# Seven half products for eight in the gate and up projections of a dense SwiGLU

## The reference, cut to what matters

```
h  = h + gated_deltanet(...)
hn = rms_norm(h, ffn_norm[0])                                  # (256, 1024)
h  = h + (silu(hn @ w_gate) * (hn @ w_up)) @ w_down            # w_gate, w_up (1024, 3584), w_down (3584, 1024)
...                                                            # layer 1: attention, then 8 experts
```

## Time and profile before

| | before |
|---|---|
| median of 3 runs (lowest to highest) | 1490.9 us (1490.5 to 1490.95) |
| span of the profiled execution | 1489.1 us |
| what lies around the span, median less span | 1.8 us |
| TensorE busy | 1477.0 us (99%) |
| VectorE, ScalarE, GpSimd busy | 1189.9, 947.9, 116.2 us |
| share of the chain that ended last | PE 96%, DVE 2%, DMA 1% |

### The profile page before, as it was taken

One profiled execution on the slowest core, in us unless ns is written; L12 is line 12 of the kernel. 1 busy time (PEld: TensorE's weight loads), 2 busy tenths in 40 slices (PEclk: granted clock), 3 DMA queues, 4 the chain that ended last, 5 costly groups with the idle time before them and its releaser, 6 DMA issues.

```text
span 1489.1 us, 20171 instructions
## 1 busy us (share of the span) xinstructions
PE 1477.0 (99%) x7900; PEld 1234.6 (83%) x7900; DVE 1189.9 (80%) x1056; ACT 947.9 (64%) x852; POOL 116.2 (8%) x77
## 2 busy tenths in 40 slices
PE   9999999999999999999999999999999999999998
PEld 7999988888887788888888888888888888888886
DVE  5977775444478699889889889898898988988985
ACT  4554544434465676777677777677777677767773
POOL 0470110000013000000000000000000000000000
PEclk9999999999999999999999999999999999999999
DMA  6331885555414299999999999999999999999990
GB/s 227 114 115 58 307 320 181 173 209 183 169 58 156 99 396 393 396 383 393 397 382 394 393 369 386 381 371 381 383 380 372 389 380 363 391 383 359 395 362 30
DMA packets 186696, 445.60 MB, mean 299 GB/s; under 512 B 5399, under 2 KB 5680, under 8 KB 186635
## 3 DMA queue, kind: packets, MB, share of 16 engines
q1 hardware_dynamic: 182208, 430.12, 77.7%
q0 software_dynamic: 3936, 14.20, 3.3%
q10 hardware_dynamic: 490, 0.42, 0.1%
HBM read 437.89 MB, written 7.89 MB: 299 GB/s over the span
## 4 chain that ended last, share of the span: by engine, by line
PE 96%; DVE 2%; DMA 1%; ACT 0%; POOL 0%; issue 0%; SPq 0%; DVEq 0%; ACTq 0%
PE bank L1482 14%; PE bank L1484 14%; PE bank L1483 14%; PE bank L1467 7%; PE bank L1469 7%; PE bank L1468 7%; PE bank L698 4%; PE bank L1145 3%; PE bank L1144 3%; PE bank L1143 3%; PE bank L785 2%; PE bank L789 2%; PE bank L790 2%; PE bank L791 2%; PE bank L1132 1%; PE bank L1130 1%
## 5 line engine op out<-in xcount | busy, mean ns | idle before, releaser
L2625 DVE TENSOR_TENSOR ring_r<-ring,buf_r 128x2048 fp32r<-128x2048 f32 x336 | 751.2, 2284 | 28.0 <-ACT buf_r L1926 28.0
L1926 ACT ACTIVATE buf_r<-ring 128x2048 fp32r<-128x2048 f32 x336 | 629.4, 1914 | 52.5 <-PE bank L1469 43.3
L1482 PE MATMUL bank<-ring_r,buf_r 128*128 128x512 f32 x896 | 354.5, 396 | 0.3 <-DVE buf_r L2745 0.3
L1484 PE MATMUL bank<-buf_r,buf_r 128*128 128x512 f32 x896 | 349.6, 390 | 0.0
L1483 PE MATMUL bank<-buf_r,buf_r 128*128 128x512 f32 x896 | 349.0, 389 | 0.0
L1484 PEld LDWEIGHTS bank<-buf_r,buf_r 128*128 128x128 f32 x896 | 168.0, 188 | 36.0
L1482 PEld LDWEIGHTS bank<-ring_r,buf_r 128*128 128x128 f32 x896 | 168.4, 188 | 33.6 <-DVE buf_r L2745 0.4
L1483 PEld LDWEIGHTS bank<-buf_r,buf_r 128*128 128x128 f32 x896 | 168.5, 188 | 33.4
L1467 PE MATMUL bank<-ring_r,buf_r 128*128 128x512 f32 x440 | 172.8, 393 | 0.1
L1469 PE MATMUL bank<-buf_r,buf_r 128*128 128x512 f32 x440 | 171.5, 390 | 0.0
L1468 PE MATMUL bank<-buf_r,buf_r 128*128 128x512 f32 x440 | 171.2, 389 | 0.0
(11 more groups left out here) (378 smaller groups left out, 1867.1 us busy)
## 6 DMA issues: line engine op xcount, KB each, us to landing
ring<-in_moe_w_gate SPq DMA_DIRECT2D x56, 2048.0 KB, 10.0
ring<-in_moe_w_up SPq DMA_DIRECT2D x56, 2048.0 KB, 10.4
ring<-in_moe_w_down SPq DMA_DIRECT2D x56, 2048.0 KB, 10.4
ring<-in_a_w_in SPq DMA_DIRECT2D x8, 2048.0 KB, 8.5
ring<-in_dense_w_gate SPq DMA_DIRECT2D x7, 2048.0 KB, 7.8
ring<-in_dense_w_up SPq DMA_DIRECT2D x7, 2048.0 KB, 7.9
ring<-in_dense_w_down SPq DMA_DIRECT2D x7, 2048.0 KB, 8.0
ring<-in_a_w_out SPq DMA_DIRECT2D x2, 2048.0 KB, 10.9
```

Of the source, the lines that this page charges most:

```text
L1482: pe.matmul(o, xh, low[:, c], start=k == 0, stop=False)
L1484: ins = pe.matmul(o, xh, high[:, c], start=False, stop=k == KT - 1)
L1926: act.activation(HB[m % NHB], half_words(m, U_MOE), ACT.Copy).then_inc(m_wh, 1)
L2625: dve.tensor_tensor(half_low(m, U_MOE), half_words(m, U_MOE), HB[m % NHB], ALU.subtract).then_inc(m_wl, 1)
```

## The change: what it does

The slices 3 to 6 are taken in pairs (3, 4) and (5, 6) (`MIXED`). For the gate of one pair, and for the up of one pair, the input is two token tiles by two halves of the 1024 input rows, and the weights are two halves by two slices. The plain way is eight half products. The new way is seven, by Strassen's method in the form with shared sums: seven weight matrices (three blocks as they are, four sums of blocks) times seven row matrices. Slices 1 and 2 (`PLAIN`) stay plain, in a new order. Dense now has 54 blocks (`NB`), 0 to 53, of 24 matmuls, or of 12 where they are one of the 28 products:

blocks 0 to 3 slice 0; 4 to 7 gates of 1 and 2; 8, 9 down 0; 10 to 13 ups of 1 and 2; **14 to 20** gate products of 3 and 4; 21, 22 down 1; **23 to 29** up products; 30, 31 down 2; **32 to 38** gate products of 5 and 6; 39, 40 down 3; **41 to 47** up products; 48 to 53 downs 4, 5, 6.

```diff
+def dense_blocks():
+    out = [("w", kind, 0, half) for kind in ("gate", "up") for half in range(2)]
+    for p in range(1, PAIRS + 1):
+        j = 2 * p - 1
+        for kind in ("gate", "up"):
+            if p in PLAIN:
+                out += [("w", kind, j + sl, half) for sl in range(2) for half in range(2)]
+            else:
+                qd = 2 * MIXED.index(p) + (kind == "up")
+                out += [("w", kind, j, 0), ("t", qd, 1), ("t", qd, 0), ("w", kind, j, 1), ("t", qd, 2),
+                        ("w", kind, j + 1, 1), ("t", qd, 3)]
+            ...                                # downs: one after the gates, one after the ups (p > 1)
+def turns_after(p):                            # the block after which each of 4 groups is turned
+    s = pair_at(p, "up")
+    if p in PLAIN:
+        return [s + 2, s + 3, s + 5, s + 6]
+    return [s + 5, s + 7, s + 8, s + 9]
 SP:
+                    if BLOCKS[m][0] == "t":
+                        sp.wait_ge(sums_done, 16 * SUMS * (BLOCKS[m][1] // 2 + 1))
+                    sp.dma_start(block_dst(m), block_src(m)).then_inc(slot_full[block_place(m)[0]], 16)
 GpSimd:
+            landed(pool, 1)
+            sums_start(0, [0, 1])              # DRAM to DRAM copies of 1 MB
             ...
             proj_low(6)
+            sums_start(0, [2, 3])
             ...                                # in the level masks: after level 3, after level 4
+                    sums_add(0, 0)             # two adding DMAs of 1 MB, DRAM to DRAM
+                    sums_add(0, 1)
+            landed(pool, 7)
+            pool.wait_ge(sums_done, 16 * SUMS)
+            sums_start(1, range(4))
             ...
+            sums_add(1, 2)                     # after the second norm's power, line 588 at 195.35 us
+            sums_add(1, 3)
+            def both_parts(qd):
+                pool.wait_ge(first_out, 2 * qd + 2)
+                pool.tensor_tensor(out, out, FIRSTP, ALU.add).then_inc(quad_p, 1)
+            def quad_hidden(p):                # SiLU(gate) x up of three of the four outputs
+                for i, (sl, t) in enumerate(((1, 1), (1, 0), (0, 1))):
+                    pool.wait_ge(part_v, 4 * qd + 2 + i)
+                    pool.tensor_tensor(QPR[:, sl, t, :], QPR[:, sl, t, :], QSG[:, sl, t, :], ALU.mult)
 TensorE (m is the first of the seven):
+                product(m, A_BANK, rows_of(0, 0), start=True)
+                ...                            # product(m + 1) waits: pr_ready >= hiddens_before(p), if p - 1 is plain
+                product(m + 1, B_BANK, mixed(1), start=True)
+                product(m + 2, C_BANK, mixed(0), start=True)
+                pe.wait_ge(first_out, 2 * qd + 1)
+                product(m + 3, A_BANK, rows_of(1, 0))
+                pe.wait_ge(part_v, 4 * qd + 1)
+                product(m + 4, B_BANK, mixed(2))
+                pe.wait_ge(first_out, 2 * qd + 2)
+                product(m + 5, C_BANK, mixed(3))
+                pe.wait_ge(part_v, 4 * qd + 2)
+                product(m + 6, B_BANK, rows_of(1, 1))
 hidden_tp: all turns of slices 1 to 6 go through one bank
+                    pe.wait_ge(ht_ready, 2 * j + t)
 VectorE, in the loop over m before dense_low(m) (s is the first of the seven):
+                if m == 10: mixed_rows()       # four sums of row blocks, once
+                if m == 13: mixed_low()
+                ... if m == after + 5: hidden_low(...)
+                    if m == s + 5: sixth_part(qd)
+                    if m == s + 7: first_hidden(qd) (up only); last_piece(qd)
+                    if m == s + 9: side_pieces(qd)
+                    if m == s - 1: second_sum(qd)      # 128x2048 float32 sum
+                    if m == s + 1: fourth_sum(qd)      # 128x2048 float32 sum
+                ... if m == pair_at(p, "up") + 5 + i: plain_hidden(p, i // 2, i % 2)
```

More of the change, by code:

```diff
@@ L68, in slot_of, with block_before, high_place, high_free @@
+def block_before(m):
+    b = max((i for i in range(m) if block_place(i) == block_place(m)), default=-1)
+    return b if b < 0 or block_loaded(b) else b - b % 2 + 1
+def high_place(m):
+    return m % 4
+def high_free(m):
+    return m - 3
 def slot_of(n):
@@ L1112, in down, with product @@
+                    if m == NB - 1:
                         ins.then_inc(d_out, 1)
[L1114 to L1117, removed]
+                return ins
+            def product(m, bank, of, start=False):
                 pe.wait_ge(d_wl, m + 1)
[L1119 to L1122, removed]
[L1123 to L1149 removed]
@@ new lines, in product @@
+                low, high = block_low(m), block_high(m)
+                for k in range(4):
+                    c = slice(k * FS, (k + 1) * FS)
+                    ah, al = of(k)
+                    pe.matmul(bk[bank][:, :], ah, low[:, c], start=start and k == 0, stop=False, skip_group_check=not start)
+                    pe.matmul(bk[bank][:, :], al, high[:, c], start=False, stop=False, skip_group_check=not start)
+                    ins = pe.matmul(bk[bank][:, :], ah, high[:, c], start=False, stop=k == 3, skip_group_check=not start)
@@ L2424, in _ @@
             rows_low(1)
-            for m in range(4, HALVES):
+            for m in range(4, NB + 4):
                 if m == 4:
-                    slice_hidden(0, 0)
-                dense_low(m)
+                    slice_hidden(0)
+                if m == 10:
+                    mixed_rows()
+                if m == 13:
+                    mixed_low()
+                for p in range(1, PAIRS + 1):
+                    for g, after in enumerate(turns_after(p)):
+                        if m == after + 5:
+                            hidden_low(2 * p - 1 + g // 2, g % 2)
+                for qd in range(QUADS):
+                    s = quad_at(qd)
+                    if m == s + 5:
+                        sixth_part(qd)
+                    if m == s + 7:
+                        if qd % 2 == 1:
+                            first_hidden(qd)
+                        last_piece(qd)
+                    if m == s + 9:
+                        side_pieces(qd)
+                    if m == s - 1:
+                        second_sum(qd)
+                    if m == s + 1:
+                        fourth_sum(qd)
+                for p in PLAIN:
+                    for i in range(4):
+                        if m == pair_at(p, "up") + 5 + i:
+                            plain_hidden(p, i // 2, i % 2)
+                if m < NB:
+                    dense_low(m)
                 if m == 4:
```

514 lines of the change are left out of this document (398 added, 116 removed).

## The result

The changed kernel takes 1503.07 us (median of 4 runs, 1500.69 to 1504.97), the one before 1490.7 us beside it. The ratio is 1.0082, 95% interval 1.0068 to 1.0097. Forecast were 1488.4 us, range 1484.5 to 1495.5: wrong in sign, and outside the range. The profiled execution has a span of 1501.0 us, 11.9 more than before.

What follows compares the result with a forecast made beforehand. TensorE was taken to bound the dense stage: 10.9 us of matmuls less, 8.4 us of stalls more, so -2.5 us on a span of 1489.1, and 1488.4 us as median against 1490.9; range 1484.5 to 1495.5.

Steps and rivals of the forecast that it cites:

- 48 matmuls: Dense stage: 960 matmuls instead of 1008, at 0.227 us each, take 10.9 us off TensorE.
- stall 1: Before product 15: TensorE waits 2.5 us for a plain product behind block 17's subtraction and a low part in VectorE's list.
- stalls 2 and 4: Turns after blocks 16 and 32: each waits 1.85 us for the previous turn's low part, behind a subtraction in VectorE's list.
- stall 3: Turn after block 30: waits 2.2 us for VectorE's list, 0.85 of it without GpSimd, 1.3 for four GpSimd operations.
- the same turn in the last pair (48): Turn after block 48: no stall in the forecast's own case; 2.3 us if GpSimd and VectorE exclude each other.
- rival B: GpSimd operations each hold VectorE up 1.25 us: stall 4.6 at block 30's turn, 2.3 at block 48's; 1493.1 us, chance 0.18.
- block 6's load: Start of dense: the load of block 6's weights lands in time despite the second set's adds, cost 0.
- rival C: Second set's adding DMAs go before the dense loads near 197 us, block 6 is 6.3 us late; 1494.7 us, chance 0.05.
- Rival A: Dense stalls are half or less of those walked, VectorE being further ahead: 1480 to 1484, say 1483 us; chance 0.19.
- the walk without GpSimd: Turn after block 30: VectorE's list alone, GpSimd taking nothing from it, makes TensorE wait 0.85 us.
- "Hidden" loads: Dense weight loads need 240 GB/s against 396 moved, with a ring 12 blocks deep: no TensorE wait on a transfer.
- The copies: Copies at 21 us, before dense, meet idle engines (3 GB/s): no cost counted.

Runs made afterwards that it cites:

- experiment 3: Changed kernel with the last plain product (slice 2, token tile 1) moved ahead of block 17's subtraction in VectorE's list: 1498.37 us, ratio 1.0056 to the kernel before.
- experiment 6: Changed kernel with the high and low parts of the turns behind blocks 15 and 31 one block earlier: 1498.01 us, ratio 1.0050 to the kernel before.
- experiment 4: Changed kernel with ten extra matmuls, their result overwritten, filling TensorE's wait before product 15 (and again before product 24): 1502.62 us, ratio 1.0081 to the kernel before.
- experiment 9: Changed kernel with GpSimd's ten dense operations on 16 columns instead of 512, most of their work left out: 1498.46 us, ratio 1.0050 to the kernel before.
- experiment 2: Changed kernel with two of the four DRAM to DRAM copies moved behind the level 2 masks: 1500.48 us, ratio 1.0064 to the kernel before.
- experiment 10: Kernel of experiment 8 with the low part of the turn after block 30 earlier and the adds one block later: 1485.82 us, ratio 0.9967 to the kernel before.
- experiment 1: Changed kernel with the second set's four adding DMAs moved together to behind block 7: 1517.82 us, ratio 1.0177 to the kernel before.
- experiment 7: Changed kernel without the second set's four adding DMAs, part of the result left out: 1498.03 us, ratio 1.0056 to the kernel before.
- experiment 8: Changed kernel with edits of experiments 3, 5 and 6, two copies earlier, second set's adds one at a time behind blocks 9 to 12: 1487.08 us, ratio 0.9978.
- experiment 5: Changed kernel with GpSimd's third product on VectorE and the parts of the turn after block 28 one block earlier: 1500.77 us, ratio 1.0060 to the kernel before.

## Why the prediction was wrong

The step that failed is the sum of the stalls as a price (8.4 us against the 10.9 that the matmuls give back): I took a stall of TensorE to cost its own length, and I took the list of stalls for complete. By its own steps, with what the runs showed:

| step | predicted us | measured us |
|---|---|---|
| 48 matmuls | -10.9 | 960 in dense at 0.227: -10.9 |
| stall 1, product 15 | 2.5 | 2.4 |
| stalls 2 and 4 | 1.85 each | 1.8 each |
| stall 3 | 2.2 | 3.1 |
| the same turn in the last pair (48) | 0 (rival B 2.3) | 0.7 |
| block 6's load | 0 (rival C 6.3) | 2.8 |
| clock behind a wait | not there | 5.1 |
| later start of dense (copies beside the input's load) | 0 | 3.6 |
| sum | -2.5 | +10.4 of +11.9 |

- **The walks were right.** Stalls 1, 2 and 4 came out within 0.1 us, and experiments 3 and 6 took them away by moving the very item that I had named. Rival A (gain stays) was wrong for the reason given.
- **A stall is not its own length.** No step asked what TensorE does after a wait. Three stretches at half clock cost 5.1 us, the largest missing term. The trace of before could not show it, where TensorE's longest wait in the earlier trace rows is 1.5 us. The distance of the matmuls (0.43 us) shows what a stretch costs, the count in experiment 4 that it comes with long waits (21 of 24), and experiment 3 what both are worth (3.8 us of dense for a wait of 2.4).
- **Stall 3 was sized by a mean.** I spread the one full collision in rows 6 and 7 over four operations, 0.3 us each. Here two of VectorE's operations in reach grew by 1.1 and 0.7, and GpSimd's last products came 4.6 us after they began, so the turn waited for them instead of for VectorE. Rival B had the mechanism and, with 4.6 at this place, the wrong size; without GpSimd's work (experiment 9) 0.2 us of this wait are left, so all but that is its doing. That my 2.2 lay within 0.9 us of the measured 3.1 was luck: the walk without GpSimd had 0.85.
- **"Hidden" loads.** The ring is 12 blocks deep, but not at the start of dense: block 6 goes into a slot that block 0 still holds, so its load went out at 215.0 us, into full engines. Rival C said that the adds go first and that block 6 lands near 230.7 us and is split by 234.9. It landed at 230.73 and was split at 235.0. The times agree by luck: I had the load standing in the queues behind the adds, and it went out only at 215.0; and TensorE, 3.6 us behind by then, waited 2.8 and not 6.3. At 0.05 its chance was far too small: my bound for an adding transfer (9.5 to 28 us) held for each add here (the last took 26.5), but I had not asked what four at once do to others.
- **The copies.** I read where the first of four copies stand in the list, with idle engines. The other two stood behind a product of GpSimd and went out at 58.7 us, just as the last inputs were loaded. Experiment 2 gives back 2.35 of the 3.6 us; with the copies at 50.8 us (experiment 10) dense starts at 200.46, as before the change.
- About 1.5 us of the 11.9 have no place yet.

Experiment 10 shows what the change is worth with these terms dealt with: 4.8 us, and not the 10.9 of the matmuls. Its dense is 5.5 us shorter than before: 4.4 us of waits are left, all on VectorE, which is busy 56.1 of 61.0 us from 284 to 345 us, and about 1 us has no place.

## What to carry over

Where a change fills an engine next to the bounding one, walk its list from block to block, and price a stall at more than its own length if it is longer than any that the kernel already has. Follow every transfer, adds in DRAM above all, to the time that it really goes out, together with the loads that are due then, and spread them one by one over stretches with slack.

## What the runs showed of the hardware

- Four adding DMAs of 1 MB, DRAM to DRAM, issued within 3 us, and the dense loads beside them kept all 16 engines full from 204 to 230 us, at 208 GB/s and then 299, the last add landing after 26.5 us; in experiment 1 after 38.4. Without the adds (experiment 7) the share from 204 to 216 us was 0.19 instead of 1.13. Issued one by one behind blocks 10 to 13 (experiment 10) they cost the loads nothing that TensorE saw: from 256 to 280 us it was busy 24.0 of 24 us. A block earlier (experiment 8) 0.8 us were lost.
- In dense, 21 of 24 TensorE waits of 2.4 us or longer came with a stretch at 1.2 GHz, and none of 16 waits of 1.0 to 2.3 us. The stretch was 3.41 us long, or 6.83 (twice in experiment 5, behind waits of 3.0 and 3.2, and once in experiment 2, behind 3.0). In the wait of 20.5 us the clock fell after 2.1 us and rose 5.5 us behind its end. Outside dense such stretches also came without a long wait (experiment 10, at 514 us).
- A GpSimd operation of 16 columns takes 0.22 us or 2.20, by what VectorE runs beside it.
